# One core's diffusion trunk: the order of the opening loads, the split of the modulation, and a modulation block moved into the norm seams

## The reference

```python
def modulate(x, g, shift, scale):
    return rmsnorm(x, g) * (1.0 + scale) + shift

for l in range(DEPTH):
    mc = adaln(c_ctx, ada_w[l], ada_b[l])     # silu(c) @ ada_w + ada_b, split in six:
    ml = adaln(c, ada_w[l], ada_b[l])         # shift, scale, gate for the mixer and for the FFN
    hc, hl = modulate(xc, norm_mix[l], mc[0], mc[1]), modulate(xl, norm_mix[l], ml[0], ml[1])
    ...                                       # retention (l = 0) or attention (l = 1)
    xc, xl = xc + mc[2] * yc, xl + ml[2] * yl
    hc, hl = modulate(xc, norm_ffn[l], mc[3], mc[4]), modulate(xl, norm_ffn[l], ml[3], ml[4])
    xc = xc + mc[5] * conv_ffn(hc, ffn_w_in[l], ...)
    xl = xl + ml[5] * conv_ffn(hl, ffn_w_in[l], ...)
```

## Time and profile before

| | |
|---|---|
| median of three runs | 2123.9 us |
| profiled execution, and its span | 2131.0 us, 2129.1 us |
| PE busy | 2032.3 us (95%) |
| PEld, DVE, ACT, POOL busy | 80%, 46%, 31%, 35% |
| HBM read, written | 185.65 MB, 7.08 MB |
| mean granted clock of TensorE | 0.977 of full |
| longest wait of PE, by line | L375 for ACT 14.8 us, L358 for ACT 11.9 us |

### The profile page before, as it was taken

The page is one execution under the profiler, slowest core; times in us unless marked ns, Lnnn a source line. Parts: engine busy times, 40 slices in busy tenths (PEclk is TensorE's granted clock), DMA queues, the critical chain, the costliest instruction groups (busy, mean ns, idle before and its releaser), DMA issues.

```text
span 2129.1 us, 29874 instructions
## 1 busy us (share of the span) xinstructions
PE 2032.3 (95%) x11176; PEld 1693.4 (80%) x11176; DVE 982.4 (46%) x1325; ACT 651.6 (31%) x1283; POOL 750.5 (35%) x519
## 2 busy tenths in 40 slices
PE   5899999999999999999999999998979999999998
PEld 3686878587678847898998898895557898998996
DVE  2511420350133036654465376655634674575475
ACT  5132222222321234332232133325534332232232
POOL 3233233233323323333333333436844333333332
PEclk8999999999999999999999999998989999999999
DMA  8322232133223211442343222330001522222221
GB/s 319 121 97 70 99 112 77 50 110 109 79 90 109 70 50 42 156 149 79 110 138 117 71 71 78 127 112 23 1 11 50 180 73 76 78 72 76 72 77 50
DMA packets 53125, 194.20 MB, mean 91 GB/s; under 512 B 5920, under 2 KB 7328, under 8 KB 52000
## 3 DMA queue, kind: packets, MB, share of 16 engines
q1 hardware_dynamic: 48096, 174.68, 25.0%
q10 hardware_dynamic: 4928, 18.08, 2.2%
HBM read 185.65 MB, written 7.08 MB: 91 GB/s over the span
## 4 chain that ended last, share of the span: by engine, by line
PE 84%; DVE 4%; issue 4%; POOL 3%; ACT 2%; DMA 2%; DVEq 1%; POOLq 0%; SPq 0%; ACTq 0%
PE ps L401 34%; PE ps L444 20%; PE ps L416 16%; PE ps L617 2%; DVE front L1271 2%; PE ps L463 2%; PE ps L626 1%; POOL w_l L1141 1%; ACT pr L1097 1%; PE ps L358 1%; DMA first_w<-first_dram 1%; PE ps L612 1%; DMA raw<-stream_dram 1%; POOL pr L1247 1%; PE ps L490 1%
## 5 line engine op out<-in xcount | busy, mean ns | idle before, releaser
L1141 POOL TENSOR_TENSOR w_l<-raw,w_h 128x1024 fp32r<-128x1024 f32 x232 | 562.9, 2428 | 1135.9 <-ACT w_h L824 1135.9
L401 PE MATMUL ps<-h_h,w_h 128*128 128x256 f32 (+1 forms) x1696 | 530.1, 313 | 4.6 <-issue 4.6
L401 PE MATMUL ps<-h_l,w_h 128*128 128x256 f32 (+1 forms) x1696 | 524.5, 309 | 0.0
L401 PE MATMUL ps<-h_h,w_l 128*128 128x256 f32 (+1 forms) x1696 | 524.2, 309 | 0.0
L824 ACT CAST w_h<-raw 128x1024 fp32r<-128x1024 f32 x232 | 245.9, 1061 | 554.9 <-PE ps L444 298.9
L401 PEld LDWEIGHTS ps<-h_h,w_h 128*128 128x128 f32 x1696 | 321.9, 190 | 19.2 <-issue 18.2
L401 PEld LDWEIGHTS ps<-h_l,w_h 128*128 128x128 f32 x1696 | 322.2, 190 | 2.1 <-issue 1.9
L401 PEld LDWEIGHTS ps<-h_h,w_l 128*128 128x128 f32 x1696 | 322.2, 190 | 0.0
L1510 DVE SCALAR_TENSOR_TENSOR cc<-ca,vec,cc 128x641 f32<-128x641 f32 x88 | 224.7, 2553 | 13.9 <-issue 12.8
L416 PE MATMUL ps<-w_h,h_h 128*128 128x512 f32 (+1 forms) x520 | 199.8, 384 | 1.0 <-issue 1.0
L416 PE MATMUL ps<-w_l,h_h 128*128 128x512 f32 (+1 forms) x520 | 198.2, 381 | 0.0
(11 more groups left out here) (189 smaller groups left out, 2708.7 us busy)
## 6 DMA issues: line engine op xcount, KB each, us to landing
raw<-stream_dram SPq DMA_DIRECT2D x312, 512.0 KB, 3.6
first_w<-first_dram SPq DMA_DIRECT2D x16, 512.0 KB, 19.6
gate<-gate_b_dram ACTq DMA_DIRECT2D x4, 1024.0 KB, 5.6
S<-state_dram ACTq DMA_DIRECT2D x4, 1024.0 KB, 7.1
new_state_dram<-st_out ACTq DMA_DIRECT2D x8, 512.0 KB, 3.1
xt<-x_dram ACTq DMA_DIRECT2D x5, 512.0 KB, 10.1
y_dram<-front SPq DMA_DIRECT2D x5, 512.0 KB, 2.6
rope_t<-rope_t_dram ACTq DMA_DIRECT2D x1, 512.0 KB, 3.5
```

The lines of the kernel that those rows point to most:

```text
L401: mm = nc.tensor.matmul(ps[:, banks + half, 0:width(half)], w, x[:, k, lo_hi(half)], start=(k == 0 and n == 0), stop=(k == KT - 1 and n == 2))
L1141: nc.gpsimd.tensor_tensor(w_l[:, r, :], raw[:, s, :], w_h[:, r, :].bitcast(F32), ALU.subtract).then_inc(raw_used[s], 1)
```

## The change

First, in the opening: both of the first two modulation blocks are loaded ahead of the stream; PE waits for each chunk of a block and not for all four; the three small tables and the gate bias are no longer loaded at the start on ACT's queue but after the first norm is done, and the decay tables are computed there, all of them; and for tiles 1 and 3 ACT applies the modulation instead of DVE. The factor of 32 (root of 1024) is multiplied into the norm weights once instead of into each `mod_a`.

Second, at the seams: one modulation block stands ahead of the first pair on PE, in bank 3, and ACT copies it; for tiles 3 and 4 ACT modulates the second half of the features. The stream's order follows ("mmaaaamm"), and so does the order of `hi`.

Third, the columns are cut at 256 instead of 384: part 0 of the first pair waits for tiles 0 and 1, part 1 for tiles 2 to 4.

All 24 activations of the tables and four DMAs now stand between the last rounding and the load of the rotary table. The diff, cut to its core:

```diff
-HALF = 3 * P
+HALF = 2 * P
...
+GATE_KINDS, ATT_KINDS = "mmaaaamm", "mmaaaammmmaaaammmmmm"
+PARTS = ((((GATE, 1), (GATE, 1), (TURN, 2)), ((TURN, 4),), ((None, 3),)),
+         (((GATE, 1), (GATE, 1), (None, 2)), ((None, 4),), ((None, 3),)))
+FFN_ADA = ({(0, 0): 12, (0, 1): 13, (0, 2): 14, (1, 0): 16}, {(0, 0): 22, (0, 1): 23})
...
+PART_TOKENS = ((0, 1), (2, 3, 4))
...
+        def f_on_act(n, t, hk):
+
+            return t in (1, 3) if n == 0 else t >= 3 and hk == 1
+
+        def wait_f(eng, n, t, hk):
+
+            on_act = f_on_act(n, t, hk)
+            before = sum(f_on_act(m, *x) == on_act for m in range(n) for x in halves(m))
+            mine = [x for x in halves(n) if f_on_act(n, *x) == on_act]
+            eng.wait_ge(f_act if on_act else f_dve, before + mine.index((t, hk)) + 1)
...
-                    sp.dma_start(first_w[:, 4 * n + kc, :], dr["first"][4 * n + kc]).then_inc(first_in[n], 16)
+                    sp.dma_start(first_w[:, 4 * n + kc, :], dr["first"][4 * n + kc]).then_inc(first_in[n][kc], 16)
 
             sp.dma_start(cst[:], dr["cst"]).then_inc(const_in, 16)
             load_first(0)
+            load_first(1)
             load(0, 0, None)
             load(1, 0, None)
-            load_first(1)
             load_first(2)
...
-            def first_tiles(b, n, o):
+            def first_tiles(b, n, o, ada):
 
                 pe.wait_ge(res_done, 10 * o + 9)
-                first_pair(b, n, 0, range(0, 2))
+                pe.wait_ge(mods_done, ada)
+                ada_block(b, 0, 0, -1)
+                first_pair(b, n, 0, range(0, 5))
                 norm_turn(n, 3)
-                first_pair(b, n, 0, range(2, 5))
+                first_pair(b, n, 0, range(5, KT))
                 norm_turn(n, 4)
-                first_pair(b, n, 0, range(5, KT))
+                pe.wait_ge(ada_copied, ada + 1)
                 first_pair(b, n, 1, range(KT))
+                pe.wait_ge(res_done, 10 * o + 10)
...
-                pe.wait_ge(first_in[n], 64)
                 pe.wait_ge(mods_done, n)
                 for k in range(KT):
+                    if k % 2 == 0:
+                        pe.wait_ge(first_in[n][k // 2], 16)
...
+                                    first_tiles(b, 1 + 2 * l, o - 1, ada0)
+                                elif mode == GATE and q == 0:
+                                    pe.wait_ge(mods_done, ada0 + i)
+                                    ada_block(b, 0, i, 0)
                                 for w in range(2):
                                     def free(half, w=w, n=n):
                                         if half == 0:
                                             pe.wait_ge(a_evac[l], 2 * n + w + 1 + 4 * i)
                                     if not (first and q == 0):
                                         feature_tile(b, 2 * q + w, i, 2 * w, free)
-                                    if mode and q == 0 and w == 0:
+                                    if mode == TURN and q == 0 and w == 0:
                                         pe.wait_ge(res_done, 10 * o)
                                         pe.wait_ge(mods_done, ada0 + i)
                                         ada_block(b, 0, i, 0)
                                     if mode and q == 0 and w == 1:
...
-            first_tiles(b, 2, 6)
-            pe.wait_ge(res_done, 10 * 7)
-            pe.wait_ge(mods_done, ATT_ADA)
-            ada_block(b, 0, 0, 0)
+            first_tiles(b, 2, 6, ATT_ADA)
+            gate_turn(0, ATT_ADA + 1)
             for j in range(2, 10):
                 def free(half, j=j):
                     if half == 0:
                         pe.wait_ge(aqk_evac, j - 1)
                 feature_tile(b, j, 0, 2 * (j % 2), free)
-                if j == 4:
+                if j == 2:
                     pe.wait_ge(mods_done, ATT_ADA + 1)
                     ada_block(b, 4, 0, 0)
-                if j in (2, 5):
-                    gate_turn(0, ATT_ADA + 1 + (j == 5))
+                if j == 3:
+                    gate_turn(0, ATT_ADA + 2)
...
-            act.dma_start(diff, dr["diff"]).then_inc(dec_in, 16)
-            act.dma_start(iota, dr["iota"]).then_inc(dec_in, 16)
-            act.dma_start(tri, dr["tri"]).then_inc(dec_in, 16)
-            act.dma_start(gate[:], dr["gate_b"][0]).then_inc(gate_in, 16)
...
+            def norm_f(n, t, hk):
+
+                x, s = half_at(n, t, hk), int(t == 0)
+                act.wait_ge(a_ready, 1 + hk if n == 0 else n + 2)
+                act.wait_ge(turned, HALVES * n + x + 1)
+                for kk in range(4):
+                    k = 4 * hk + kk
+                    op = nc.scalar.activation(scaled_x[:, t, k * P:(k + 1) * P], ps[:, 5 + x % 3, kk * P:(kk + 1) * P],
+                                              ACT.Identity, scale=mod_a[:, k, s:s + 1],
+                                              bias=mods[:, 16 * n + k, s:s + 1])
+                op.then_inc(f_act, 1)
...
+                ada_copy(SEG[NEXT_OF[n]], 0, 0, 3)
                 for t in (3, 4):
+                    norm_f(n, t, 1)
                     for hk in range(2):
                         norm_hi(n, t, hk)
-                    hi(b, tiles - 5 + t + RING, 0)
+                for j in (tiles - 2, tiles - 1):
+                    hi(b, j + RING, 0)
...
-            act.wait_ge(dec_lg, 1)
-            act.wait_ge(dec_in, 48)
-            act.wait_ge(const_in, 16)
...
-            decay_tables(0)
             hi(b0, 0, 0)
             hi(b0, 1, 0)
-            for t in range(TT):
-                norm_hi(0, t, 0)
-            hi(b0, 2, 0)
-            hi(b0, 3, 0)
+            for hk in range(2):
+                norm_f(0, 1, hk)
+                norm_hi(0, 0, hk)
+                norm_hi(0, 1, hk)
+                norm_f(0, 3, hk)
+                for t in range(2, TT):
+                    norm_hi(0, t, hk)
+                if hk == 0:
+                    hi(b0, 2, 0)
+                    hi(b0, 3, 0)
+            act.dma_start(diff, dr["diff"]).then_inc(dec_in, 16)
+            act.dma_start(iota, dr["iota"]).then_inc(dec_in, 16)
+            act.dma_start(tri, dr["tri"]).then_inc(dec_in, 16)
+            act.wait_ge(dec_lg, 1)
+            act.wait_ge(dec_in, 48)
+            decay_tables(0)
             decay_tables(1)
             nc.scalar.activation(small[:, 56:64], small[:, 40:48], ACT.Exp, scale=float(P)).then_inc(dec_exp, 1)
-            for t in range(TT):
-                norm_hi(0, t, 1)
+            act.dma_start(gate[:], dr["gate_b"][0]).then_inc(gate_in, 16)
             act.dma_start(rope_t[:], dr["rope_t"]).then_inc(rope_in, 16)
...
-                V.tensor_scalar(mod_a[:, ks, :], mod_a[:, ks, :], float(D) ** 0.5, None, ALU.mult)
-                dve.drain()
 
             def norm_f(n, t, hk):
 
+                if f_on_act(n, t, hk):
...
+            V.tensor_scalar(norm_g, norm_g, float(D) ** 0.5, None, ALU.mult)
...
-                    parts += [w_in[[t, FT + t]], w_in[[t + 1, FT + t + 1]]]
+                    pair = [w_in[[t, FT + t]], w_in[[t + 1, FT + t + 1]]]
                     if mode:
-                        parts.append(next(blocks))
+                        pair.insert(1 if mode == GATE else 2, next(blocks))
+                    parts += pair
...
-            parts += [wq[0:4], ada1[16:20], wq[4:8], ada1[20:24], wk]
+            parts += [wq[0:2], ada1[16:20], wq[2:6], ada1[20:24], wq[6:8], wk]
```

81 lines of the change are left out of this document (45 added, 36 removed).

## The result

The changed kernel takes 2095.7 us (median of 4 executions, 2094.1 to 2103.6), the kernel before 2122.5 (4 executions, 2118.9 to 2126.5). The profiled executions give nearly the same: spans of 2129.1 and 2101.7 us.

The account below looks back on a forecast made before the run. TensorE was taken as busy nearly throughout, with idle and half-clock stretches at the opening and norm seams. Seams 11.3 plus opening 1.1 gave 12.4 us off 2123.9, the median of before: 2111.5 us, range 2102 to 2120.

Parts of the forecast that it names:

- a wait of 2.25 us inside the pair: At each seam, PE was to wait 2.0 us for tile 4 at part 1 of the pair; bounds 1 and 3.3.
- the second half near 48: In the opening, modulation of the second half of the features was to start at 48.4 us instead of 58.5.
- PE held by the rotary table: In the opening, PE was to idle some 10 us before the first gate's turn, for DVE's copy behind the rotary table.
- The start of the block: At a seam, PE was to start the modulation block at 833.9, when DVE had written tile 3 of the residual.
- The opening: Up to the first gate's turn: 4.2 us earlier, less 3.1 for half rate, a gain of 1.1; bounds -1.4 to 5.2.
- The clock at the seams: Half rate behind the new wait inside the pair, counted as half of three times 1.7: a loss of 2.5 us.
- 13.8: Forecast gain in us over the three seams, 4.3, 5.2 and 4.3, before the loss to the clock.
- A: Rival: the opening's tail does not hold PE, which turns the gate near 64; 13 us more gained, 2098.5; chance 0.07.
- B: Rival: the new wait inside each pair is 3.3 us, each followed by half rate; 5.9 us gained, 2118; chance 0.20.
- C: Rival: the block in the gap waits for its own chunks, 3 us late per seam; 3.4 gained, 2120.5; chance 0.10.
- D: Rival: second blocks of each FFN and the attention wait for their last chunk; 26 us lost, 2137.5; chance 0.06.
- The rule on ACT's operands: ACT's four modulations at a seam: 1.2 us by the nearest row, used in the sum; about 1.6 by the skill.

Follow-up runs that it names:

- E3: The kernel before with only its columns cut at 256 instead of 384; ratio 0.9927, 14.6 us faster.
- E9: The changed kernel, but the modulation block in the gap waits for the tenth residual (tile 4's) instead of the ninth (tile 3's); 2103.2 us, ratio 0.9904.
- E8: The changed kernel, unchanged, profiled a second time; span 2094.5 us.
- E13: The changed kernel, unchanged, profiled a third time and timed again; 2098.2 us, ratio 0.9874.
- E5: The changed kernel with the old cut at 384 columns, all else of the change kept; 2107.2 us, ratio 0.9920.
- E1: The kernel before with only the change's opening, seams and cut as they were; 2115.2 us, ratio 0.9969.
- E16: The kernel before with only the change's opening, profiled again; opening 85.5 us, seams 407.7 us.
- E10: The changed kernel, but ACT loads and computes the decay tables between the first norm's halves, and DVE awaits the rotary table only after its first gate addition; 2092.0 us.
- E6: The changed kernel, but DVE modulates both halves of tiles 3 and 4 at the seams and ACT only rounds; 2096.3 us, ratio 0.9871.

## Why the prediction was wrong

The direction was right, and so were most mechanisms of the forecast: the block in the stretch that was idle before, a wait of 2.25 us inside the pair (2.0), the gate directly behind it, the second half near 48 (48.4), PE held by the rotary table (9.7 us against about 10; it was 3.9 and 7.2 in the two later profiles, so that the nearness is luck). The sum was half of what came. The steps that failed:

**The start of the block, 3 x 1.3 us.** "PE may start the block when DVE has written tile 3 of the residual, at 833.23 + 0.69" took the wrong row. The residuals of the second half, tiles 0 to 4, are five rows. The first four are

```profile
819.88 0.69 DVE L1318 TENSOR_TENSOR xt<-ps,xt 128x512 f32<-128x512 f32 x1
...
822.63 0.69 DVE L1318 TENSOR_TENSOR xt<-ps,xt 128x512 f32<-128x512 f32 x1
...
825.38 0.69 DVE L1318 TENSOR_TENSOR xt<-ps,xt 128x512 f32<-128x512 f32 x1
...
829.31 0.69 DVE L1318 TENSOR_TENSOR xt<-ps,xt 128x512 f32<-128x512 f32 x1
```

and the fifth is 833.23, which is tile 4's. The code waits for the ninth of ten, at 829.31: done before PE's turn of tile 2 ends at 832.70. So the block needs no wait, PE has none ahead of it, and each seam is 1.3 us shorter than worked out. E3 shows the same from the other side: with the cut alone the pair starts right behind the turn, and nothing of the 3.29 us is left. E9 puts the forecast's wait in: 1.26 us of idle at the first seam, 3.6 us over the three, and 5.4 with the half rate.

**The opening, 4 to 5 us.** Forecast 1.1, measured 5.2 in the first profiles, 6.3 over all. ACT's last rounding was on time (53.7 against 54.1); the term that was too large is the time of the issues behind it. They ran ahead of ACT's own work. The three small loads were issued from 52.20 on, before the last rounding began. The gate's load was issued at 60.98 and the rotary table's at 61.35, while the last activation of the tables began at 63.64, and I had put them behind 65.5. The landing was sized rightly on average: counted from the gate's issue, as the 7.6 us of the earlier trace rows are, the rotary table held DVE for 9.5 us here, 6.1 in E8 and 7.6 in E13. So DVE went on at 70.5 (67.1 and 68.2 in the others) and not at 73.1: the turn is 78.19 - 71.23 = 7.0 us earlier and not 4.2. The half rate behind the idle lasted 3.6 us, 1.8 lost and not 3.1, which leaves the 5.2:

```profile
71.20:74.80 3.60, 3.56 (x5) 1.51 (x5) 0.00 (x0) 0.00 (x0) 1.80 (x1) 0.50 1.00 414
```

**The retention, 4 us, not in the sum at all.** The earlier trace rows was taken as an example of an idle piece, and I did not ask whether it would recur. It is a stall with a fetch of instructions that the kernel before pays twice in each of three profiles and the changed one twice in three profiles together; each costs its idle, and the longer ones 1.7 us of clock besides. This makes about 3.1 of the 4.2 us. The other 1.1 is half rate behind the wait near the retention's end, which fell out differently from profile to profile: luck of these executions.

**The clock at the seams, 1 us.** I took off 2.5 us. In the three profiles after, the stretch behind the wait was at half clock at two, one and none of the three seams, 1.7 us each, so 1.7 on average. With 13.8 + 3.9 - 1.7 = 16.0 the seams' 17.1 is nearly met; the last 1.1 us is not accounted for.

**The rivals.** A (the opening's tail does not hold PE) was wrong, the tail held it for 4 to 10 us in all three profiles after; its time, 2098.5, came out near for another reason. B's wait was 2.25 and not 3.3. C and D did not come: no wait of PE for chunks at the block, and none above 0.4 us at the second blocks.

**The cut was no by-matter.** The forecast priced it as the reason for the new wait. E3 and E5 show it as about half of the gain: alone it brings 14.6 us, and the change without it 16.8 (beside its own runs of before), so that it adds 9.9 to the rest, of 26.7. In the opening the new cut and the new order do not add up: 86.8 by the one, 86.8 by the other (means of two), 86.5 to 90.0 by both. With the new order the tail of ACT's queue holds PE under either cut, 3.6 to 6.5 us with the old one alone (E1, E16) and 3.9 to 9.7 in the changed kernel. E10 frees that and gets 78.3 and 80.9.

**The rule on ACT's operands.** The four modulations with scale and bias took 1.50 us, where the nearest row of before made 1.2. The Trainium skill, ScalarE: Activation LUTs, What ACT_TABLE_LOAD costs, says about 93 ns for each per-partition pointer; by that they were estimated at 1.6, and the trace is nearer to it. E6 shows that the difference weighs nothing.

## What to carry to other kernels

A wait on a counter names a number: find in the trace the row that brings the counter to it, by counting the rows, before a time is taken from it; the wrong row cost 3.9 us here. Where a pair of stages starts on the first tiles, cut so that the first part needs only tiles that are long ready, and put the part with the late tiles behind other work. When work is deferred to a queue's tail, look for that queue's idle stretch in the middle of the same stage (here 10.7 to 11.5 us on ACT) and put it there. Try each part of a change alone: here one number, the cut, was worth 10 to 15 us of 27, and the new order of the opening nothing beside it until its tail was moved.
